# High and low activation halves laid side by side, chunk by chunk, at an offset of 128 bytes, in a hybrid decoder step

## What is computed

```
h = rms_norm(x)
q, kc, vc, ks, vs, kw, vw, gn, u, v, ga, gb = split(h @ w_in)
o_a = nsa_attend(...)                       # compressed, selected and window attention
o_b = gmlp_spatial(gelu(u), gelu(v), ...)
x += (sigmoid(ga) * (o_a @ w_branch_a) + sigmoid(gb) * (o_b @ w_branch_b)) @ w_out
x += cross_attend(rms_norm(x) @ w_cq, memory) @ w_co
x += (silu(h2 @ w_gate) * (h2 @ w_up)) @ w_down      # h2 = rms_norm(x), hidden width 2816
y = rms_norm(x)
```

## The kernel before

| | hi | lo | high weights, slot 0 | low weights, slot 0 |
| --- | --- | --- | --- | --- |
| mix (w_in) | 93728 | 127520 | 169504 | 173600 |
| mid (branches, w_out, w_cq), tail (w_co, gate, up) | 170976 | 137184 | 217056 | 212960 |
| a (w_down) | 93728 | 110624 | 217056 | 212960 |

## Time and profile before

### The profile page before, as it was taken

The page is one execution under the profiler, slowest core; times in us unless marked ns, Lnnn a source line. Parts: engine busy times, 40 slices in busy tenths (PEclk is TensorE's granted clock), DMA queues, the critical chain, the costliest instruction groups (busy, mean ns, idle before and its releaser), DMA issues. The chain is left out here.

```text
span 2214.8 us, 38450 instructions
## 1 busy us (share of the span) xinstructions
PE 2118.7 (96%) x14076; PEld 1962.7 (89%) x14076; DVE 929.5 (42%) x1958; ACT 551.1 (25%) x1151; POOL 611.8 (28%) x531
## 2 busy tenths in 40 slices
PE   7999999988989999799999988999999999999998
PEld 6999999965855767599999878999999999999997
DVE  4111111186336676455661346563333333333335
ACT  5002211122326655222030332221111111111112
POOL 2233322245224444412212322212212122121220
PEclk9999999999979999899999999999999999999999
DMA  6212222394323000544212432110211112111121
GB/s 199 55 47 62 72 90 93 127 262 151 90 62 136 1 2 1 142 146 146 85 39 67 191 120 62 46 49 29 67 31 55 48 33 62 33 53 48 33 62 78
DMA packets 206648, 175.77 MB, mean 79 GB/s; under 512 B 25867, under 2 KB 186348, under 8 KB 205963
## 3 DMA queue, kind: packets, MB, share of 16 engines
q1 hardware_dynamic: 197450, 152.96, 22.7%
q10 hardware_dynamic: 4448, 11.81, 1.5%
q0 software_dynamic: 4640, 9.61, 1.5%
HBM read 147.02 MB, written 27.39 MB: 79 GB/s over the span
## 5 line engine op out<-in xcount | busy, mean ns | idle before, releaser
L152 POOL TENSOR_TENSOR tail_w_lo<-mem_last_slot,tail_w_hi 128x1024 fp32r<-128x1024 f32 (+1 forms) x94 | 183.3, 1950 | 689.8 <-ACT tail_w_hi L140 689.8
L191 PE MATMUL ff_psum<-tail_hi,tail_w_hi 128*128 128x352 f32 x1056 | 341.2, 323 | 1.0 <-PEq L2112 1.0
L192 PE MATMUL ff_psum<-tail_lo,tail_w_hi 128*128 128x352 f32 x1056 | 338.5, 321 | 0.0
L193 PE MATMUL ff_psum<-tail_hi,tail_w_lo 128*128 128x352 f32 x1056 | 338.2, 320 | 0.0
L191 PE MATMUL bank<-mix_hi,in_w_hi 128*128 128x352 f32 x840 | 271.9, 324 | 1.3 <-issue 1.3
L192 PE MATMUL bank<-mix_lo,in_w_hi 128*128 128x352 f32 x840 | 270.0, 321 | 0.0
L193 PE MATMUL bank<-mix_hi,in_w_lo 128*128 128x352 f32 x840 | 269.9, 321 | 0.0
L140 ACT CAST tail_w_hi<-mem_last_slot 128x1024 fp32r<-128x1024 f32 (+1 forms) x94 | 81.2, 863 | 509.3 <-PE ff_psum L193 433.4
L191 PEld LDWEIGHTS ff_psum<-tail_hi,tail_w_hi 128*128 128x128 f32 x1056 | 198.1, 188 | 2.0 <-issue 1.5
L192 PEld LDWEIGHTS ff_psum<-tail_lo,tail_w_hi 128*128 128x128 f32 x1056 | 198.4, 188 | 0.1
L193 PEld LDWEIGHTS ff_psum<-tail_hi,tail_w_lo 128*128 128x128 f32 x1056 | 197.9, 187 | 0.0
(11 more groups left out here) (394 smaller groups left out, 3822.2 us busy)
## 6 DMA issues: line engine op xcount, KB each, us to landing
in_raw<-w_in SPq DMA_DIRECT2D x70, 256.0 KB, 3.2
mem_last_slot<-w_gate SPq DMA_DIRECT2D x44, 256.0 KB, 3.2
mem_last_slot<-w_up SPq DMA_DIRECT2D x44, 256.0 KB, 3.3
mem_last_slot<-w_down SPq DMA_DIRECT2D x80, 128.0 KB, 2.2
gate_kept<-x_first ACTq DMA_DIRECT2D x16, 528.0 KB, 2.7
uv<-gate_kept SPq DMA_DIRECT2D x16, 528.0 KB, 4.6
mem_ring<-cache_mem_v SPq DMA_DIRECT2D x8, 1024.0 KB, 13.2
mem_ring<-cache_mem_k SPq DMA_DIRECT2D x7, 1024.0 KB, 7.0
```

Of the source, the lines that this page charges most:

```text
L152: pool.tensor_tensor(lo, raw, hi.bitcast(F32), ALU.subtract).then_inc(self.split, 1)
L191: pe.matmul(out, hi, x_hi, start=k == 0, stop=False)
L192: pe.matmul(out, hi, x_lo, start=False, stop=False)
L193: last = pe.matmul(out, lo, x_hi, start=False, stop=k == len(terms) - 1)
```

## The change

High and low halves become one tensor of [c, k, half, 352 positions] in each partition: the high part of block k and chunk c, behind it the low part of the same block and chunk, then the next k, and chunk after chunk. The start of block (c, k, half) is 1408 x (2 (8 c + k) + half) bytes from the tensor's start (4 in place of 8 for a). The tensor is made 32 elements (128 bytes) longer. In mix this moves the weights up by 128 bytes, since they are placed behind it; in mid and tail the tensor is placed from the right end and begins at 137056; in a it begins 128 bytes later, at 93856, with the weights where they were. The last product with w_down keeps its position pieces: for it the tensor is read as a high and a low half of [k, T] as before. Instructions, their number and their order on each engine stay as they are; only addresses differ.

```diff
+SHIFT = 32
...
 def products(ps, hi, lo, depth=KD):
-    return lambda b, c: [(ps[b][:, 0:C], 0, [(hi[:, k, cols(c)], lo[:, k, cols(c)]) for k in range(depth)])]
+    return lambda b, c: [(ps[b][:, 0:C], 0, [(hi[:, c, k], lo[:, c, k]) for k in range(depth)])]
+
+def side_by_side(sb, ctx, name, depth):
+
+    n = 2 * CH * depth * C
+    both = sb(ctx, f"{name}_hi_lo", [P, n + SHIFT], F32R)[:, 0:n].rearrange("p (c k h t) -> p c k h t", c=CH, k=depth, h=2)
+    return both[:, :, :, 0], both[:, :, :, 1]
...
     def round(self, act, c):
         for k in range(KD):
-            hi, x = self.hi[:, k, cols(c)], self.src[k][:, cols(c)]
+            hi, x = self.hi[:, c, k], self.src[k][:, cols(c)]
...
-            return sb(ctx, f"{name}_hi", [P, KD, T], F32R), sb(ctx, f"{name}_lo", [P, KD, T], F32R)
+            return side_by_side(sb, ctx, name, KD)
...
-                    hi, lo = (sb_right(wide, f"mid_{x}", [P, KD, T], F32R) for x in ("hi", "lo"))
+                    hi, lo = side_by_side(sb_right, wide, "mid", KD)
...
-            hi, lo = (sb_right(tail, f"tail_{x}", [P, KD, T], F32R) for x in ("hi", "lo"))
+            hi, lo = side_by_side(sb_right, tail, "tail", KD)
...
-        a_hi, a_lo = (sb(ctx, f"a_{x}", [P, FF_DEPTH, T], F32R) for x in ("hi", "lo"))
+        n = 2 * FF_DEPTH * T
+        a = sb(ctx, "a_hi_lo", [P, n + SHIFT], F32R)[:, SHIFT:SHIFT + n]
+        a_hi, a_lo = (a.rearrange("p (c k h t) -> p c k h t", c=CH, k=FF_DEPTH, h=2)[:, :, :, h] for h in range(2))
+        a = a.rearrange("p (h x) -> p h x", h=2)
...
+        last_hi, last_lo = (a[:, h].rearrange("p (k t) -> p k t", t=T)[:, 0:last_size] for h in range(2))
...
-                        to_hi, to_lo = (flat(x[:, bass.ds(it + n, 1), cols(c)]) for x in (a_hi, a_lo))
+                        if f == last_f:
+                            to_hi, to_lo = (flat(x[:, bass.ds(it + n, 1), cols(c)]) for x in (last_hi, last_lo))
+                        else:
+                            to_hi, to_lo = (flat(x[:, c, bass.ds(it + n, 1)]) for x in (a_hi, a_lo))
```

More of the change, by code:

```diff
@@ L419, in rest @@
         for k in range(KD):
-            hi, lo, x = self.hi[:, k, cols(c)].bitcast(F32), self.lo[:, k, cols(c)], self.src[k][:, cols(c)]
+            hi, lo, x = self.hi[:, c, k].bitcast(F32), self.lo[:, c, k], self.src[k][:, cols(c)]
             dve.wait_ge(self.rounded, KD * c + k + 1)
@@ L766, in _ @@
                     for k in range(KD):
-                        act.mul(hi[:, k, cols(c)], xT[:, k, cols(c)], gains[:, g, k:k + 1]).then_inc(rounded, 1)
+                        act.mul(hi[:, c, k], xT[:, k, cols(c)], gains[:, g, k:k + 1]).then_inc(rounded, 1)
                 square_rows(1)
@@ L843, in _ @@
                         dve.wait_ge(rounded, KD * c + k + 1)
-                        dve.scalar_tensor_tensor(lo[:, k, cols(c)], xT[:, k, cols(c)], gains[:, g, k:k + 1],
-                                                 hi[:, k, cols(c)].bitcast(F32), ALU.mult, ALU.subtract).then_inc(split, 1)
+                        dve.scalar_tensor_tensor(lo[:, c, k], xT[:, k, cols(c)], gains[:, g, k:k + 1],
+                                                 hi[:, c, k].bitcast(F32), ALU.mult, ALU.subtract).then_inc(split, 1)
                 keep_roots(0)
@@ L2058, in _ @@
                 groups = lambda b, c: [
-                    (ps[2 * b + m][:, 0:C], 4 * m, [(hi[:, 4 * m + k, cols(c)], lo[:, 4 * m + k, cols(c)]) for k in range(4)]) for m in range(2)]
+                    (ps[2 * b + m][:, 0:C], 4 * m, [(hi[:, c, 4 * m + k], lo[:, c, 4 * m + k]) for k in range(4)]) for m in range(2)]
                 for m in range(2):
@@ L2323, in _ @@
                     pe.wait_ge(st.freed, st.sets + last_q + max(q - 3, 0))
-                    st.terms(pe, n // 4, [(ps[q % 4][:, 0:t1 - t0], last_size * (n % 4), [(a_hi[:, k, t0:t1], a_lo[:, k, t0:t1]) for k in range(last_size)])])
+                    st.terms(pe, n // 4, [(ps[q % 4][:, 0:t1 - t0], last_size * (n % 4), [(last_hi[:, k, t0:t1], last_lo[:, k, t0:t1]) for k in range(last_size)])])
                     if q in TURN_AFTER:
```

## The result

The changed kernel takes 2243.5 us (median of 4 runs, 2241.0 to 2249.1), the kernel before 2215.5 us beside it: ratio 1.0125, 95% interval 1.011 to 1.0141. It is 28 us slower; forecast were 18 us less. The time lies outside the range.

What follows compares the result with a forecast made beforehand. TensorE's interval between wide matmuls was taken to bound the kernel. Parity and joined runs together, 1.9 ns a matmul, including the down product, gave 18 us less: 2214.8 - 18 = 2197 us, range 2174 to 2232.

Steps and rivals of the forecast that it cites:

- What bounds the kernel: Wide stages: the interval between matmuls, 159.3 ns x 9432, sets 1502 us of 2214.8; each ns is paid in full.
- Parity from matmul to matmul: Wide matmuls: 128-byte start parity becomes odd, even, odd for every k, 320.0 ns against 320.9, 8 us less.
- Runs that join: Low half starts where the high half ended; bounded between nothing beyond parity's 8 us and 27 us less, middle 18 taken.
- The down product: Its 1440 matmuls, starting 64 bytes off the multiples, get the same 1.9 ns less, between 0 and 5.
- The repeated parity costs: Rival: third matmul of each k and first of the next repeat parity; 3.1 ns more, +29 us, 2244 us; chance 0.21.
- Nothing changes: Rival: differences between starts only move about, their mean stays, time 2215 us; chance 0.16.
- All of it goes: Rival: new distances avoid all conflicts of the two streams, interval falls to 150 ns, 88 us less, 2127 us; chance 0.06.

Runs made afterwards that it cites:

- The chain: Matmuls alone, decoder left out, with set address steps; d is activations' distance from high weights modulo 256 bytes; the new layout takes 157.7 to 164.3 ns.
- the layout without any repetition: Changed kernel with high and low halves as two tensors, each chunk by chunk, no shift: 2227.5 us, ratio 1.004 to the kernel before.
- the worst distances: Changed kernel with low weights 128 bytes off the high ones and 128 bytes behind them, both slots alike: 2258.5 us, ratio 1.0177 to the kernel before.

## Why the prediction was wrong

**What bounds the kernel: right.** The wide interval is what the time follows, each ns of it is paid in full, and no other engine, wait or queue became the bound. Idle time and the other engines' durations stayed, as forecast. Interval = duration - 162 ns held too: 324 and 162.

**Parity from matmul to matmul: the step that failed.** It priced the new triple at 320.0 ns by adding one price per kind of step, and took odd to odd from the earlier trace rows as 320. (The six durations before average 321.0, not 320.9; that is 9 us in place of 8 and changes nothing.) Measured, the three lines of tail are 323, 324, 325, mean 324: the triple costs 3 ns more where 0.9 less was forecast. By the same table the layout without the shift (even, odd, even: 318, 322 and 323) would be the dearer, 321.0. The chip has it the other way: 322 without the shift, 324 with it. The chain shows why such a table can't be read from rows of before: with fixed addresses, odd to odd for ever takes 166.7 ns an interval in one place and 158.3 in another. The odd-to-odd steps of the earlier trace rows sit in a sequence that changes parity every three matmuls. The price of a step is not a property of the step; the sequence settles into a rhythm with a mean of its own, which depends on all three distances and, in some settings, on what ran before. The term was -8 us; in its place the layout alone brought +8 us (no shift) and the shift on top of it some +20.

**Runs that join: no such gain.** The term was -10 us on no row. In the chain the joined runs at d 128 take 162.2 ns and fixed addresses with the same distances, which don't join, 162.3.

**The down product: sign wrong.** It went from 160.3 to 161.3 ns, 1 ns x 1440 = 1.4 us more, where 1.9 ns a matmul, 2.7 us, less was forecast.

**The rivals.** "The repeated parity costs" had the size almost exactly, 2244 us, and the matmuls in the window, fewer than 550, came as it said; yet the number is luck in good part. Without the shift every k repeats the parity too, so the rival gives 2244 us for it as well, and the time is 2225; and the layout without any repetition takes 2227.5. What decides in the new layout is which distances are repeated., with a mean of 324, were the only rows read before that showed an interval of 162 ns. "Nothing changes" is out: from 157.8 to 164.4 ns in the same stage, with equal instructions, by addresses alone. With it goes what the prediction read out of the Trainium skill's "SBUF — State Buffer", section Who interferes with whom (two independent read ports, and TensorE never waits on anyone), that no distance to the weights could matter. Whether the ports themselves interfere, no run shows. "All of it goes": the best of 16 settings for the new layout still has 157.7 ns, so the excess over 150 ns shrinks by some 1.5 ns and does not go. The Trainium skill's "TensorE: Matmul & The Clock Gate", section Back-to-back issue gap, from which the prediction had its estimate of 149.2 ns, gives that formula for a single matmul by itself. For a stream in which each has its weight load it says 131 ns at 512 columns. Neither fits this stream: 157.7 ns at 352 columns is the least of any setting, and 512 columns take 226.7.

What stays open is the mechanism below the addresses. That moving stream and weight stream disturb each other at the memory is argued from the dependence on their distance, not shown. Why the interval follows these distances modulo 256 bytes, which of several rhythms a stretch falls into, and why fixed addresses 256 bytes apart (128 and 384) can differ by 8 ns, no run tells.

## What to carry to other kernels

When a kernel's time is a count times an interval, measure that interval in a bare chain with the real addresses before choosing a layout: the chain gave the whole kernel's interval within 0.3 ns in each stage in which all tiles have the same distances and keep one rhythm, and picked a placement worth 12 us with no instruction changed. It did not foresee the stage that alternates between two rhythms. Prices taken from single steps of an alternating sequence don't carry over to a sequence that repeats one of them. A layout whose step is a multiple of 256 bytes repeats one set of distances for good or ill, so its distances between activations, high weights and low weights have to be chosen together, and for every buffer slot.

## What was not expected of the hardware

- The interval of an fp32r matmul of 352 columns depends on where in a partition the things it reads start, in the main on their distances modulo 256 bytes: 157.7 to 166.7 ns with identical shapes at the full granted clock.
- Single intervals of such a stream are unequal and follow a pattern that lasts for hundreds of matmuls: 161, 162, 156, 161, 155, 159 ns before, 167, 167, 159, 168, 166, 159 with the worst distances.
- One sequence can have more than one lasting pattern: the same settings gave 160.1 and 162.2 ns behind different predecessors, and the two-tensor kernel 158.9 and 161.1 ns in alternate pieces of one stage.
- Narrow fp32r matmuls have a floor: 128 and 192 columns both take 111.7 ns with a weight load before each.
